# Bucket masks of five groups made in the short convolution, in two-byte form, and their table matmuls in the second convolution layer

## Chip, core and metric

The kernel is one program on one core of a Trainium2 chip. The metric is the device time of one execution in microseconds (us), of which the median of three runs is taken. PE is TensorE, DVE is VectorE, ACT is ScalarE, POOL is GpSimd and SP is SyncE, which issues the loads of weights.

## What is computed

Two networks run one after the other on a sequence of 256 tokens of width 1024: four mixer layers (conformer convolution "a0", forgetting attention "b", short convolution "c", conformer convolution "a1"), then two blocks of token mixer and feed-forward ("m0", "f0", "m1", "f1"). The change touches the first three kinds and one small thing that the token mixers need, the table of position biases. Cut from the reference:

```python
def conformer_conv_mixer(h, w_in, conv_w, conv_b, ln_g, ln_b, w_out):
    val, glu_gate, z = jnp.split(h @ w_in, 3, axis=-1)
    u = causal_depthwise_conv(val * jax.nn.sigmoid(glu_gate), conv_w) + conv_b   # 31 taps
    u = jax.nn.silu(layer_norm(u, ln_g, ln_b))
    return (u * jax.nn.silu(z)) @ w_out

def short_conv_mixer(h, w_in, conv_w, w_out):
    u, b_gate, c_gate, z = jnp.split(h @ w_in, 4, axis=-1)
    y = b_gate * causal_depthwise_conv(c_gate * u, conv_w)                       # 3 taps
    return (y * jax.nn.silu(z)) @ w_out

bias = rel_bias[t5_bucket(q_pos[:, :, None] - k_pos)]      # 32 buckets, 8 heads, in dsa_attention
```

The kernel writes the bias as a sum of steps: for every bucket a mask says whether the distance of a query and a key has reached the bucket's start, and a matmul of the masks with the differences of neighbouring rows of `rel_bias` gives the bias.

## The kernel before

**Pieces.** The weights come as one stream of pieces of 128x1024 (512 KB), loaded by SP into six `raw` buffers in the order of a fixed plan. A "plain" piece is multiplied as it is (fp32, records of `ps<-B,raw`). A "split" piece is first rounded by ACT into one of five `wh` buffers (CAST `wh<-raw`), DVE makes the rest (`wl<-raw,wh`, a TENSOR_TENSOR of 128x1024), and PE multiplies both (`ps<-XS,wh` and `ps<-XS,wl`, 24 matmuls for a piece of an input projection; `ps<-wh,os` and `ps<-wl,os`, 12 for a piece of an output projection). `feed_act` and `feed_dve` call these up to three pieces ahead of the piece that they name. A cast waits for the load and for the matmuls of the split piece that held its `wh` buffer before. Pieces called ada are used by DVE alone (`raw<-raw,cb`), in c and later.

**A conformer layer** (`pe_a`, `act_a`, `dve_a`, `pool_a`) works in eight rounds p = 0 to 7 of 256 channels. In round p PE multiplies the pair g(p) (plain, the gates), the pair v(p) (split from p = 1 on, the values) and, from p = 1, one unit of z (plain up to z3); each round of the plan so has five pieces g, g, v, v, z, and v(p+2).0 takes the `wh` buffer of v(p+1).0. ACT takes the sigmoid (`gate`), DVE multiplies (`val`, `B<-ps,tmp`), and then the round's 31 taps run: ACT scales 12 of them per half (`tmp<-B,C`, in pairs, into three buffers `tmp2` to `tmp4` in turn) and POOL adds them (`B<-B,tmp`, 24 a round), DVE does 17 (`ps<-B,C,ps`, 34 a round) and ends the round with `conv_end` (`B<-ps,B`). ACT and DVE run "items" n = 0 to 29 of a round p, with the work for later pieces put between them by hand: the cast of v(p+1).1 follows item 3, the gate of p+1 item 9, the cast of v(p+2).0 item 13, in even rounds the Silu of z behind it, `stats(p-1)` (a Square, `tmp<-B`) item 17, and the next point used below item 21. ACT has by item 13 scaled five of its twelve taps, by item 21 nine. PE sums the squares in `stats` (`ps<-B,C` and `ps<-tmp,C`, 32x256).

**The table of biases** is made in six groups e = 0 to 5. `masks` on DVE makes four masks y of a group (TENSOR_TENSOR `B<-B`, 128x512), `pe_bias` multiplies them (four matmuls side by side, 32 columns each, `ps<-B,C` 32x512), `act_bias_out` copies the result to `G`, `pe_bias_turn` transposes it (four `ps<-C,G`), and `act_bias` puts it in its place (`B<-ps`, 128x512). Groups 0, 1 and 2 are made in a0 and 3, 4 and 5 in a1: DVE makes four masks ahead of the rounds, and four more in rounds 2 of a0 and 1 and 4 of a1, since all groups use one set of mask buffers and wait for the group before:

```python
            if e:
                dve.wait_ge(*s["table"][e - 1])      # masks: the matmuls of the group before
        if e:
            pe.wait_ge(*s["evac"]["bias", e - 1])    # pe_bias: act_bias of the group before (bank 3)
```

A group's `act_bias` stands one round behind its `pe_bias` in ACT's order, and its turn two rounds behind in PE's.

**The short convolution** c (`pe_c`, `act_c`, `dve_c`) has eight steps i = 0, 2, ... 14 of the pieces c, c, u, u, b, b, o(i-2), z, z, o(i-1), with ada pieces between. DVE multiplies by `ps5` once u is there, runs the taps, multiplies by `ps6` once b is there, and later by the Silu of z; the rests `wl` are fed between these.

## Time and profile before

| | |
|---|---|
| median of three runs (lowest, highest) | 1817.43 us (1815.01, 1819.13) |
| span of the profiled execution | 1817.8 us |
| PE, DVE, ACT, POOL busy | 1747.3, 1446.8, 1075.3, 331.3 us |
| share of the span | 96%, 80%, 59%, 18% |
| mean granted TensorE clock | 0.989 |
| a0, b, c, a1, the rest | from about 0, 245, 521, 756 and 997 us on |

The profiled execution has no time of its own outside the profile; its span lies within the three timed runs. POOL's 18% is an average over a program in which it works in two stretches alone, the rounds of a0 and of a1, so its share there has to be read from windows of these rounds. Busy time of PE counts a matmul from its start to a modelled end, so that 96% says that PE seldom stands still, not that it runs at its peak.

### The profile page before, as it was taken

The numbers are of one execution on the slowest core, as the hardware profiler recorded it, in microseconds if no ns is written. First come the engines' busy times: TensorE is split into PE (matmuls) and PEld (weight loads), VectorE is DVE, ScalarE is ACT, GpSimd is POOL, SyncE is SP. The second block draws the span as 40 slices with busy tenths as digits, with TensorE's granted clock in tenths as the row PEclk, the third lists the DMA queues.
The fourth block names the chain that finished last, engine by engine and source line by source line (L and its number), as shares of the span: only waits on it lengthen the run. The fifth ranks groups of instructions, "written<-read, shape, count | busy, mean of one in ns | idle before, by whom it ended". The sixth has DMA issues, their size and how long they took to land.

```text
span 1817.8 us, 30986 instructions
## 1 busy us (share of the span) xinstructions
PE 1747.3 (96%) x11636; PEld 1580.2 (87%) x11636; DVE 1446.8 (80%) x2710; ACT 1075.3 (59%) x2047; POOL 331.3 (18%) x412
## 2 busy tenths in 40 slices
PE   7998999999999999999989999999999999999997
PEld 6887778888889999988877989989999898989996
DVE  7999777877778878789977688787777778787667
ACT  6888575555454444468975556565555556565554
POOL 2999000000000000079950000020000300030000
PEclk9999999999999999999989999999999999999998
DMA  6444458864558888644335554445764443536552
GB/s 228 150 141 151 140 170 310 275 204 167 197 195 278 301 295 291 208 156 151 132 128 185 169 195 135 166 152 192 242 211 161 154 148 125 176 131 220 190 182 70
DMA packets 92741, 339.62 MB, mean 187 GB/s; under 512 B 10288, under 2 KB 10672, under 8 KB 91952
## 3 DMA queue, kind: packets, MB, share of 16 engines
q1 hardware_dynamic: 92592, 337.64, 55.2%
q8 instruction: 93, 1.52, 0.3%
q14 instruction: 56, 0.46, 0.1%
HBM read 336.55 MB, written 1.05 MB: 186 GB/s over the span
## 4 chain that ended last, share of the span: by engine, by line
PE 62%; DVE 15%; issue 10%; ACT 10%; POOL 2%; DMA 1%; SPq 0%; DVEq 0%; ACTq 0%; POOLq 0%
PE ps L103 60%; DVE wl L119 6%; ACT tmp L109 4%; ACT wh L112 2%; POOL B L119 2%; DVE B L119 2%; PE ps L106 2%; DVE tmp L129 1%; ACT B L109 1%; ACT os L112 1%; DVE raw L129 1%; DVE tmp L119 1%; ACT ps L109 1%; ACT XS L112 1%; DVE os L119 1%
## 5 line engine op out<-in xcount | busy, mean ns | idle before, releaser
L103 PE MATMUL ps<-XS,wh 128*128 128x256 f32 x4464 | 830.2, 288 | 10.6 <-DVE wl L119 9.4
L103 PEld LDWEIGHTS ps<-XS,wh 128*128 128x128 f32 x4464 | 707.4, 194 | 26.5 <-issue 14.3
L119 DVE TENSOR_TENSOR wl<-raw,wh 128x1024 fp32r<-128x1024 f32 x481 | 593.4, 1260 | 111.8 <-ACT wh L112 110.7
L103 PE MATMUL ps<-XS,wl 128*128 128x256 f32 x2232 | 636.1, 285 | 0.0
L112 ACT CAST wh<-raw 128x1024 fp32r<-128x1024 f32 x481 | 486.8, 1045 | 150.2 <-PE ps L103 140.7
L103 PEld LDWEIGHTS ps<-XS,wl 128*128 128x128 f32 x2232 | 432.1, 194 | 0.0
L119 POOL TENSOR_TENSOR B<-B,tmp 128x237 f32<-128x237 f32 (+11 forms) x384 | 287.1, 785 | 644.5 <-ACT tmp L109 644.4
L103 PE MATMUL ps<-wh,os 128*128 128x512 f32 x864 | 284.1, 394 | 12.6 <-DVE os L119 8.4
L129 DVE SCALAR_TENSOR_TENSOR ps<-B,C,ps 128x254 f32<-128x254 f32 (+16 forms) x544 | 211.7, 467 | 6.8 <-ACT ps L109 6.7
L103 PEld LDWEIGHTS ps<-wh,os 128*128 128x128 f32 x864 | 162.4, 188 | 51.9 <-DVE os L119 13.2
L103 PE MATMUL ps<-B,raw 128*128 128x256 f32 x832 | 183.9, 381 | 0.9 <-ACT B L109 0.9
L103 PEld LDWEIGHTS ps<-B,raw 128*128 128x128 f32 x832 | 157.1, 190 | 26.6 <-issue 4.2
L103 PE MATMUL ps<-wh,XS 128*128 128x512 f32 x576 | 179.5, 391 | 0.0
L109 ACT ACTIVATE tmp<-B,C 128x237 f32<-128x237 f32 (+11 forms) x384 | 158.8, 477 | 26.7 <-POOL B L119 26.2
L103 PE MATMUL ps<-wl,os 128*128 128x512 f32 x432 | 168.9, 391 | 0.0
L119 POOL TENSOR_TENSOR X<-X,B 128x512 f32<-128x512 f32 x24 | 44.0, 1848 | 658.0 <-DVE XS L119 657.0
L129 DVE SCALAR_TENSOR_TENSOR tmp<-ps,C,tmp 128x254 f32<-128x254 f32 (+1 forms) x176 | 72.6, 475 | 75.9 <-ACT tmp L109 75.9
L103 PEld LDWEIGHTS ps<-wh,XS 128*128 128x128 f32 x576 | 107.2, 188 | 21.5
L109 ACT ACTIVATE tmp<-ps 128x128 f32<-128x128 f32 (+3 forms) x178 | 73.2, 427 | 77.6 <-PE ps L103 60.8
L129 DVE SCALAR_TENSOR_TENSOR raw<-raw,cb 128x1024 f32<-128x1024 f32 x96 | 116.4, 1218 | 0.0
L109 ACT ACTIVATE tmp<-ps,C 128x256 f32<-128x256 f32 x88 | 44.9, 560 | 117.9 <-PE ps L103 117.9
L103 PE MATMUL ps<-wl,XS 128*128 128x512 f32 x288 | 112.3, 390 | 0.0
(157 smaller groups left out, 1621.6 us busy)
## 6 DMA issues: line engine op xcount, KB each, us to landing
raw<-in_w SPq DMA_DIRECT2D x628, 512.0 KB, 4.4
B<-in_ln SPq DMA_DIRECT2D x4, 1024.0 KB, 6.0
C<-in_cst SPq DMA_DIRECT2D x1, 1103.5 KB, 10.2
X<-in_x SPq DMA_DIRECT2D x2, 512.0 KB, 5.6
out_x<-X SPq DMA_DIRECT2D x4, 256.0 KB, 2.5
cb<-in_cb SPq DMA_DIRECT2D x1, 512.0 KB, 12.8
pos<-in_pos SPq DMA_DIRECT2D x1, 160.0 KB, 2.3
raw<-in_w SPq DMA_DIRECT2D x1, 128.0 KB, 3.0
```

Source lines behind the costliest of these rows:

```text
L103: return NOTHING if self.e is None else self.e.matmul(*a, **k)
L106: return NOTHING if self.e is None else self.e.transpose(*a)
L109: return NOTHING if self.e is None else self.e.activation(*a, **k)
L112: return NOTHING if self.e is None else self.e.copy(*a)
L119: return NOTHING if self.e is None else self.e.tensor_tensor(o, a, b, op)
L129: return self.e.scalar_tensor_tensor(out=o, in0=a, scalar=s, in1=b, op0=op0, op1=op1, **k)
```

## The change

Group 0 stays where it is. The masks of groups 1 to 5 (20 of them) are made in c, one behind each of three places of a step (steps 0 to 12; the last place in steps 0 to 10). All masks are in two-byte form, and every one has a place of its own, so that none waits for a table. The differences of `rel_bias` are split at the start into three two-byte parts, and a group's table is 12 two-byte matmuls in place of 4 in fp32. The tables of groups 1 to 5 are all in a1, group p+1 in round p = 0 to 4: `pe_bias` behind v(p), `act_bias_out` behind item 3 of ACT's round p, the turn behind g(p+1), `act_bias` behind item 21 of the same round p. a0 keeps nothing but group 0.

```diff
@@ -785,31 +785,31 @@
             ins.then_inc(s["sums"].up((A, q)), 1)
 
         def table(p):
-            if p in self.bias_at(j):
-                self.pe_bias_turn(pe, self.bias_at(j)[p], 3)
+            if j and 1 <= p <= 5:
+                self.pe_bias_turn(pe, p, 3)
 
         for p in range(8):
             pair("g", p)
             if j == 0 and p == 0:
                 self.pe_bias_turn(pe, 0, 7)
-            table(p - 2)
+            table(p)
             if p >= 3:
                 stats(p - 3)
             pair("v", p)
-            if p in self.bias_at(j):
-                self.pe_bias(pe, self.bias_at(j)[p], 3)
+            if j and p < 5:
+                self.pe_bias(pe, p + 1, 3)
             if 1 <= p < 7:
                 pair("z", (p - 1) // 2, ((p - 1) % 2,))
         pair("z", 3)
         stats(5)
-        table(6)
         pair("z", 4)
         stats(6)
         pair("z", 5)
         pair("z", 6, (0,))
         stats(7)
         pe.wait_ge(*s["evac"][A, "S"])
-        pe.wait_ge(*s["evac"]["bias", 5 if j else 2])
+        if j:
+            pe.wait_ge(*s["evac"]["bias", 5])
         for b in range(2):
             ins = pe.matmul(self.ps[3][:, b:4:2], self.tmp[4][:, 128 * b:128 * b + 128], self.c("which", 0, 2), start=True,
                             stop=True)
@@ -899,6 +899,8 @@
                 self.feed_act(act, f"{A}.v{p + 1}.1", 0)
             if p == 7:
                 self.feed_act(act, f"{A}.z5.0", 0)
+            if j and p < 5:
+                self.act_bias_out(act, p + 1, 3)
             items(p, 4, 10)
             if p < 7:
                 gate(p + 1)
@@ -910,13 +912,11 @@
             if p in (2, 4, 6):
                 silu_z(p // 2 - 1)
             items(p, 14, 18)
-            if p in self.bias_at(j):
-                self.act_bias_out(act, self.bias_at(j)[p], 3)
             if p:
                 stats(p - 1)
             items(p, 18, 22)
-            if p - 1 in self.bias_at(j):
-                self.act_bias(act, self.bias_at(j)[p - 1], 3)
+            if j and p < 5:
+                self.act_bias(act, p + 1, 3)
             if p >= 6:
                 self.feed_act(act, f"{A}.z{2 * p - 8}.1", 0)
             items(p, 22, 30)
@@ -1004,30 +1004,24 @@
             dve.tt(U[:, a:a + 2, :].rearrange("p a t -> p (a t)"), self.ps[bank["v", p]], self.tmp[p % 2],
                    ALU.mult).then_inc(s["conv"].up((A, "v", p)), 1)
 
-        self.masks(dve, 4)
         self.feed_dve(dve, f"{A}.v1.0", 1)
         val(0)
         for p in range(8):
-            more = 1 if p in ((1, 4) if j else (2,)) else 0
             items(p, 0, 8)
             if p:
                 conv_end(p - 1)
-            self.masks(dve, more)
             if 1 <= p < 7:
                 self.feed_dve(dve, f"{A}.v{p + 1}.1", 0)
             if p == 7:
                 self.feed_dve(dve, f"{A}.z5.0", 0)
             items(p, 8, 14)
-            self.masks(dve, more)
             if p == 7:
                 self.feed_dve(dve, f"{A}.z5.1", 0)
             items(p, 14, 20)
-            self.masks(dve, more)
             if p < 7:
                 val(p + 1)
             self.feed_dve(dve, f"{A}.v{p + 2}.0" if p < 6 else f"{A}.z{2 * p - 8}.0", 0)
             items(p, 20, 28)
-            self.masks(dve, more)
             if p >= 6:
                 self.feed_dve(dve, f"{A}.z{2 * p - 8}.1", 0)
             items(p, 28, 30)
@@ -1150,11 +1144,19 @@
 
     def mask(self, y):
 
-        return self.m["B"][0][:, 2048 + y % 4 * 512:2560 + y % 4 * 512]
-
-    def bias_at(self, j):
-
-        return {0: 3, 3: 4, 6: 5} if j else {1: 1, 4: 2}
+        n = y - 4 if y >= 4 else y
+        if n < 16:
+            place = self.B[1 if y >= 4 and n < 8 else 0][:, 2048 + n % 8 * 256:2304 + n % 8 * 256]
+        elif n < 18:
+            place = self.B[2][:, 3392 + 256 * (n - 16):3648 + 256 * (n - 16)]
+        else:
+            place = self.m["G"][:, 512 + 256 * (n - 18):768 + 256 * (n - 18)]
+        return place.bitcast(BF16)
+
+    def bias_steps(self):
+
+        r = self.m["rep"][3][:].bitcast(BF16)
+        return [r[:, 32 * k:32 * k + 32] for k in range(3)]
 
     def bias_turned(self):
 
@@ -1168,6 +1170,13 @@
         dve.wait_ge(*s["const0"][0])
         dve.tt(self.c("rblk", 0, 32), self.c("rblk", 0, 32), self.c("rblk0", 0, 32), ALU.subtract).then_inc(
             s["bias"].up("steps"), 1)
+        rest = self.c("rblk", 0, 32)
+        for k, o in enumerate(self.bias_steps()):
+            dve.wait_ge(*s["bias"][("rest", k - 1) if k else "steps"])
+            dve.tensor_copy(o, rest).then_inc(s["bias"].up(("part", k)), 1)
+            if k < 2:
+                dve.wait_ge(*s["bias"]["part", k])
+                dve.tt(rest, rest, o, ALU.subtract).then_inc(s["bias"].up(("rest", k)), 1)
         dve.wait_ge(*s["bias"]["pf"])
         dve.ts(pf[:, T:T + 64], pf[:, T:T + 64], self.c("bstart"), None, ALU.add, None).then_inc(s["bias"].up("begin"), 1)
         dve.wait_ge(*s["bias"]["begin"])
@@ -1184,7 +1193,7 @@
             q, g = (0, 16 * e) if e < 2 else (128, 16 * (e - 2))
             g += T + y % 4
             if e:
-                dve.wait_ge(*s["table"][e - 1])
+                dve.wait_ge(*s["table"][0])
             dve.tt(self.mask(y).rearrange("p (c q) -> p c q", c=4),
                    pf[:, q:q + 128].unsqueeze(1).to_broadcast([128, 4, 128]),
                    pf[:, g:g + 13:4].unsqueeze(2).to_broadcast([128, 4, 128]), ALU.is_ge).then_inc(s["mask"].up(y), 1)
@@ -1192,14 +1201,14 @@
     def pe_bias(self, pe, e, bank):
 
         s = self.s
-        pe.wait_ge(*s["bias"]["steps"])
+        pe.wait_ge(*s["bias"]["part", 2])
         for g in range(4):
             pe.wait_ge(*s["mask"][4 * e + g])
         if e:
             pe.wait_ge(*s["evac"]["bias", e - 1])
-        for g in range(4):
-            ins = pe.matmul(self.ps[bank][32 * g:32 * g + 32, :], self.c("rblk", 0, 32), self.mask(4 * e + g), start=True,
-                            stop=True)
+        for k, part in enumerate(self.bias_steps()):
+            for g in range(4):
+                ins = pe.matmul(self.ps[bank][32 * g:32 * g + 32, :], part, self.mask(4 * e + g), start=k == 0, stop=k == 2)
         ins.then_inc(s["table"].up(e), 1)
 
     def act_bias_out(self, act, e, bank):
@@ -1688,6 +1697,7 @@
             dve.wait_ge(*s["gemm"][f"c.u{i}.1"])
             dve.wait_ge(*s["evac"]["c", "c", i])
             dve.tt(cs, self.ps[5], cs, ALU.mult).then_inc(s["evacd"].up(("c", "u", i)), 1)
+            self.masks(dve, 1 if i < 14 else 0)
             for n in range(2):
                 self.feed_dve(dve, f"c.b{i}.{n}")
             dve.wait_ge(*s["evacd"]["c", "u", i])
@@ -1703,6 +1713,7 @@
             dve.wait_ge(*s["gemm"][f"c.b{i}.1"])
             dve.wait_ge(*s["conv"]["c", i + 1, 2])
             dve.tt(ac, self.ps[6], ac, ALU.mult).then_inc(s["evacd"].up(("c", "b", i)), 1)
+            self.masks(dve, 1 if i < 14 else 0)
             if i >= 2:
                 self.feed_dve(dve, f"c.o{i - 2}")
             for n in range(2):
@@ -1714,6 +1725,7 @@
             dve.tt(ac, ac, zs, ALU.mult).then_inc(s["conv"].up(("c", "y", i)), 1)
             for k in range(2):
                 self.dve_low(dve, "c", i + k, ac[:, k * T:k * T + T])
+            self.masks(dve, 1 if i < 12 else 0)
         self.feed_dve(dve, "c.o14")
         self.feed_dve(dve, "c.o15")
 
```

**ACT, round 2 of a1**, from the gate to item 21 (`G<-ps3` is `act_bias_out`, `B2<-ps3` is `act_bias`, `tmp5<-B1` is `stats`; the number behind a name is the buffer's). Before:

```order
L109 ACTIVATE tmp1<-ps4 128x512 [waits s_gemm]
...
L112 CAST wh3<-raw4 128x1024 [waits s_gemm,s_raw4]
L109 ACT_TABLE_LOAD
L109 ACTIVATE B0<-ps7 128x512
...
L109 ACTIVATE tmp5<-B1 128x512 [waits s_sums,s_conv]
...
L109 ACTIVATE tmp4<-B3,C 128x229 [waits s_poolconv]
L109 ACTIVATE tmp4<-B3,C 128x229
L109 ACTIVATE tmp2<-B3,C 128x228 [waits s_poolconv]
```

Now:

```order
L109 ACTIVATE G<-ps3 128x512 [waits s_table]
...
L109 ACTIVATE tmp1<-ps4 128x512 [waits s_gemm]
...
L112 CAST wh3<-raw4 128x1024 [waits s_gemm,s_raw4]
L109 ACT_TABLE_LOAD
L109 ACTIVATE B0<-ps7 128x512
...
L109 ACTIVATE tmp5<-B1 128x512 [waits s_sums,s_conv]
...
L109 ACTIVATE tmp4<-B3,C 128x229 [waits s_poolconv]
L109 ACTIVATE tmp4<-B3,C 128x229
L109 ACTIVATE B2<-ps3 128x8x64 [waits s_turn]
L109 ACTIVATE tmp2<-B3,C 128x228 [waits s_poolconv]
```

Every round from 0 to 4 now has both copies, and `act_bias` stands behind the cast of v(p+2).0 (`wh3`), which waits for the matmuls of v(p+1).0.

**PE, a1, from the end of v(1) to the start of v(2)** (`ps7<-B3,raw3` is the unit of z, `ps5<-B3,raw4` and `raw5` are g(2)). Before:

```order
L103 MATMUL ps4<-XS,wl4 128x256
L103 MATMUL ps7<-B3,raw3 128x256 [waits s_raw3]
L103 MATMUL ps7<-B3,raw3 128x256 x7
L103 MATMUL ps5<-B3,raw4 128x256 [waits s_raw4,s_conv]
L103 MATMUL ps5<-B3,raw4 128x256 x7
L103 MATMUL ps5<-B3,raw5 128x256 [waits s_raw5]
L103 MATMUL ps5<-B3,raw5 128x256 x7
L106 MATMUL ps3<-C,G 128x128 [waits s_evac]
L106 MATMUL ps3<-C,G 128x128 x3
L103 MATMUL ps6<-XS,wh3 128x256 [waits s_low,s_cast]
```

Now:

```order
L103 MATMUL ps4<-XS,wl4 128x256
L103 MATMUL ps3<-B1,rep3 32x512 [waits s_mask,s_evac]
L103 MATMUL ps3<-B1,rep3 32x512 x11
L103 MATMUL ps7<-B3,raw3 128x256 [waits s_raw3]
L103 MATMUL ps7<-B3,raw3 128x256 x7
L103 MATMUL ps5<-B3,raw4 128x256 [waits s_raw4,s_conv]
L103 MATMUL ps5<-B3,raw4 128x256 x7
L103 MATMUL ps5<-B3,raw5 128x256 [waits s_raw5]
L103 MATMUL ps5<-B3,raw5 128x256 x7
L106 MATMUL ps3<-C,G 128x128 [waits s_evac]
L106 MATMUL ps3<-C,G 128x128 x3
L103 MATMUL ps6<-XS,wh3 128x256 [waits s_low,s_cast]
```

The 12 matmuls of a table, of which the first waits for `s_evac` (the `act_bias` of the group before) have come in ahead of z and g; the same rows stand behind v(2), v(3) and v(4), and those behind v(0) without the wait for `s_evac`. Rounds 1 to 5 each have a turn.

**DVE, a step of c**, from the product with `ps5` to the rest of the first z piece, now (before, the same rows without the two `B1<-B2`, which are masks):

```order
L119 TENSOR_TENSOR tmp0<-ps5,tmp0 128x512 [waits s_evac,s_gemm]
L119 TENSOR_TENSOR B1<-B2 128x512
L129 SCALAR_TENSOR_TENSOR raw1,mod<-raw1,cb 128x1024 [waits s_raw1]
L119 TENSOR_TENSOR wl3<-raw2,wh3 128x1024 [waits s_cast]
L129 SCALAR_TENSOR_TENSOR raw3,mod<-raw3,cb 128x1024 [waits s_raw3]
...
L119 TENSOR_TENSOR tmp2<-ps6,tmp2 128x512 [waits s_conv,s_gemm]
L119 TENSOR_TENSOR B1<-B2 128x512
L119 TENSOR_TENSOR wl0<-raw4,wh0 128x1024 [waits s_cast]
```

Both stand ahead of the rest `wl0` of z(i).0, which is the next `wl` that PE needs after the output piece o(i-2). The third mask of a step follows the two `os` of the step's end.

## Rows read from the trace of the kernel before

**Rows 1.** Windows of rounds of a0 and a1: busy us (instructions), clock, DMA.

```profile
69.34:88.74 19.40, 19.22 (x122) 16.34 (x120) 19.40 (x39) 17.11 (x38) 18.72 (x26) 1.00 0.43 143
106.09:127.05 20.96, 20.73 (x122) 18.19 (x121) 18.28 (x43) 16.84 (x38) 17.43 (x26) 1.00 0.45 151
800.78:819.92 19.14, 18.63 (x115) 16.34 (x114) 19.14 (x39) 15.52 (x36) 19.14 (x25) 1.00 0.44 147
819.92:837.28 17.36, 15.09 (x87) 13.17 (x88) 17.36 (x41) 15.57 (x37) 17.36 (x26) 0.90 0.36 122
```

**Rows 2.** Timeline, two POOL additions (a mask, and no mask beside them) and masks on DVE.

```profile
818.83 1.13 POOL L119 TENSOR_TENSOR B<-B,tmp 128x226 f32<-128x226 f32 x1
810.48 0.68 POOL L119 TENSOR_TENSOR B<-B,tmp 128x231 f32<-128x231 f32 x1
...
818.27 1.15 DVE L119 TENSOR_TENSOR B<-B 128x512 f32<-128x512 f32 x1
767.62 2.49 DVE L119 TENSOR_TENSOR B<-B 128x512 f32<-128x512 f32 x4
```

**Rows 3.** Timeline, waits in a0: DVE, PE, ACT, POOL, each [idle <-releaser].

```profile
9.16 0.17 DVE L124 TENSOR_SCALAR sm<-sm 128x2 f32<-128x2 f32 x1 [2.99 <-ACT tmp L109]
93.97 0.36 PE L103 MATMUL ps<-XS,wh 128*128 128x256 f32 x1 [2.09 <-DVE wl L119]
113.85 1.05 ACT L112 CAST wh<-raw 128x1024 fp32r<-128x1024 f32 x1 [2.34 <-PE ps L103]
117.25 34.65 POOL L119 TENSOR_TENSOR B<-B,tmp 128x232 f32<-128x232 f32 x48 [3.53 <-ACT tmp L109]
```

**Rows 4.** Windows behind two waits of PE, and the second wait in the timeline.

```profile
94.00:98.00 4.00, 4.00 (x21) 4.00 (x22) 4.00 (x12) 4.00 (x10) 4.00 (x7) 0.58 0.42 135
882.00:884.00 2.00, 2.00 (x19) 1.97 (x17) 2.00 (x7) 2.00 (x5) 2.00 (x4) 1.00 0.76 254
...
881.06 0.36 PE L103 MATMUL ps<-XS,wh 128*128 128x256 f32 x1 [1.45 <-DVE wl L119]
```

**Rows 5.** Timeline of PE in a1 (z and g, a turn, half of `stats`, a table), and the window of one v pair (v4).

```profile
791.46 10.52 PE L103 MATMUL ps<-B,raw 128*128 128x256 f32 x48
801.82 0.60 PE L106 MATMUL ps<-C,G 128*128 128x128 f32 x4
819.19 0.41 PE L103 MATMUL ps<-B,C 128*32 128x256 f32 x2
829.67 1.06 PE L103 MATMUL ps<-B,C 128*32 128x512 f32 x8
...
841.79:847.81 6.02, 6.02 (x53) 6.02 (x50) 5.32 (x14) 4.10 (x9) 4.37 (x7) 1.00 0.72 264
```

**Rows 6.** Timeline of ACT in rounds 0, 1, 2 and 4 of a1.

```profile
789.47 1.05 ACT L112 CAST wh<-raw 128x1024 fp32r<-128x1024 f32 x1 [2.21 <-DMA raw<-in_w]
808.31 0.61 ACT L109 ACTIVATE tmp<-B 128x512 f32<-128x512 f32 x1
811.33 0.57 ACT L109 ACTIVATE B<-ps 128x512 f32<-128x512 f32 x1
824.81 1.28 ACT L109 ACT_TABLE_LOAD   x1
826.60 1.61 ACT L109 ACTIVATE tmp<-B,C 128x232 f32<-128x232 f32 x4
865.19 1.61 ACT L109 ACTIVATE tmp<-B,C 128x232 f32<-128x232 f32 x4
```

**Rows 7.** Timeline of a step of c, DVE, and the start of z on PE.

```profile
621.19 0.69 DVE L119 TENSOR_TENSOR tmp<-ps,tmp 128x512 f32<-128x512 f32 x1 [1.84 <-PE ps L103]
...
627.20 0.69 DVE L119 TENSOR_TENSOR tmp<-ps,tmp 128x512 f32<-128x512 f32 x1
627.80 3.49 DVE L119 TENSOR_TENSOR wl<-raw,wh 128x1024 fp32r<-128x1024 f32 x3
...
629.50 0.40 PE L103 MATMUL ps<-XS,wh 128*128 128x256 f32 x2
```

## Prediction, made before the changed kernel was run

> **What bounds the kernel now.** I read the stages first (the windows), then who waited for whom in the conformer layers a0 and a1 (waits, timeline), then the chain that ended last, which runs through POOL, ACT and DVE in those two layers and through PE nearly everywhere else.
>
> In the rounds of a0 and a1 POOL is never idle unless it is starved. A round without a mask and without a starving wait takes 17.36 us, and POOL is busy for all of it; a round with four masks takes 19.14, again all busy; two rounds of a0 take 19.40 and 20.96, of which POOL is idle for 0.7 and 3.5 [rows 1]. So POOL's 24 additions a round set the pace, and three things slow them. (1) A mask beside an addition: that addition takes 1.13 us instead of 0.68, and the mask 1.15 instead of its 0.62 (2.49 for four) [rows 2]. (2) DVE, made late by masks, makes `wl` late: PE waits 2.09 us. (3) PE, late, holds back ACT's cast for 2.34 us, and behind the cast stand the taps for which POOL then waits 3.53 us [rows 3]. PE has hardly any slack there: z and g take 10.5 us, a v pair 6.0, `stats` 0.6 (two halves of 0.41 that overlap), so 17.1 of a round's 17.4, and a turn costs 0.5 and a table 1.0 on top (their rows say 0.60 and 1.06, and the next matmul starts within the last part of each) [rows 5]. A wait of PE costs more than itself when it is long: in the 4 us behind the 2.09 us wait the granted clock was 0.58 on average, that is mostly its lower level (1.2 GHz), behind one of 1.45 it stayed 1.00 (2.4 GHz) [rows 4]. 4 us at 0.58 lose 4 x (1 - 0.58) = 1.7; I take 1.5 for such a wait.
>
> In c PE has no idle time, and DVE's chain is short of slack at one place of each step (below).
>
> **Start.** Five small operations on the 32 columns of `rblk` come ahead of the first masks, and the first table becomes two-byte. The small operation of this stage on DVE takes 0.17 us, so five that wait for each other take about 1.0 by my estimate, and DVE then stands idle for 2.99 before ACT's squares are there [rows 3]: hidden, 0. It would take five operations of 0.6 to get past that.
>
> **a0: 8 masks, 2 tables, 2 turns, 4 copies go.** The four masks ahead of the rounds stand where DVE waits for PE or ACT anyway: 0. The four in round 2 cost POOL 4 x 0.45 = 1.8 us, and the idle 0.7 goes too: the round falls from 19.40 to 17.36. Round 4's 3.53 us wait came from PE being 2.34 late. PE gets earlier by the 2.09 wait, the slow stretch of 1.5, two tables of 1.0 and a turn of 0.5, 6.1 in all; ACT asks 2.0 earlier; 6.1 - 2.0 exceeds 2.34, so the wait goes and the round falls from 20.96 to 17.36. Sum -2.0 - 3.6 = **-5.6 us**. What follows the rounds waits for them and moves as a whole. Bounds: -2.0 if another wait takes the place of the second, -5.8 if the last idle 0.15 goes too.
> The Trainium skill (SBUF — State Buffer, "Who interferes with whom") says that a DVE operation with two SBUF inputs and a GpSimd operation that reads SBUF share a port, and that the loser is blocked until the other is done; the trace agrees in kind, 1.13 against 0.68. By that rule a mask could cost POOL its full 0.62 and not 0.45, and a0 would win 0.7 us more. I keep the row.
>
> **c: 20 masks of 0.62 us come.** POOL is idle here, so nobody shares. DVE's step has idle time (1.84 us before the product with `ps5`), but between 621.8 and the end of the first `wl` of three at about 629.0 there is next to none: the rows follow each other, and PE starts on that `wl` at 629.50 [rows 7]. Two masks stand in this stretch, 1.25 us against a slack of 0.5. PE is late by about 0.65 (0.55 to 0.75, slack of other steps being up to 0.2 more), and since DVE's next product waits for PE again, every step pays anew. Step 0 has no output piece and is looser; steps 2 to 12 pay: 6 x 0.65 = **+4 us**. Bounds: 0 if the slack is larger than the rows show, +7.5 if nothing hides. The third mask falls into a wait for a cast (under 0.1).
>
> **a1: 12 masks go, 3 tables become 5, 3 turns 5, 6 copies 10.** Without anything new this would gain: four masks fewer in round 1 and in round 4 (19.14 to 17.36). But `act_bias` of group p+1 now stands in ACT's round p behind the cast of v(p+2).0, and PE's table of group p+2, right behind v(p+1), waits for it. The cast itself waits for v(p+1).0 on PE. So there is a closed chain: table, z and g, turn, `stats`, v(p+1).0, cast, taps six to nine with the Square among them, `act_bias`, next table. I take 0.7 for a two-byte table. No row shows one; the four 32-column groups of an fp32 table plainly run side by side (1.0 us for four matmuls of 512 columns), so three parts should stand between a part's 0.25 x 3 and the fp32 price. Bounds: 0.65 (a little under the row's 1.0), and 12 x 0.25 = 3.0 if the twelve run one after another.
>
> ACT, from the start of the cast at time c: 0.95 to the next instruction, four pairs of taps at 0.77 (1.61 for four taps, two pairs), the Square 0.5, `act_bias` 0.5 = 5.0; in even rounds the table load and Silu of z add 1.8 (824.81 to 826.60) [rows 6]. PE, from table to the end of v(p+1).0: 0.7 + 10.5 + 0.5 + 0.6 + 3.0 = 15.3. One turn of the chain so takes 20.3 us in an odd round and 22.1 in an even one, against 17.4 now.
> - Round 0: the cast starts at 789.2 (789.47 now [rows 6]; g(1), whose end releases its load, ends 0.3 earlier with the cheaper table). Round 0 has no Square, so `act_bias(1)` ends at 789.2 + 0.95 + 3.1 + 0.5 = 793.7. PE ends v(1) at 791.8 (z now starts at 791.46 [rows 5], less 0.3 and with a turn of 0.5 ahead), and waits 1.9 us.
> - The cast of round 1 starts at 793.7 + 0.7 + 10.5 + 0.5 + 3.0 = 808.4, that of round 2 at 808.4 + 20.3 = 828.7, of round 3 at 828.7 + 22.1 = 850.8, of round 4 at 850.8 + 20.3 = 871.1.
> - In each PE, which ends v(p+1) 3.0 us behind c, waits for `act_bias`: 2.0, 3.8 and 2.0 us.
> - Round 4's taps go on at 871.1 + 0.95 + 1.8 = 873.9, now 865.19 [rows 6]: 8.7 late. The rest of the round no longer holds three masks, 3 x 0.45 = 1.35. **+7.4 us**.
> - The clock: the wait of 3.8 us surely lets it fall, +1.5. The three of 1.9 to 2.0 lie between 1.45 (no fall) and 2.09 (fall); I count one, +1.5. Together **+3 us** (1.5 to 6).
> After group 5 nothing waits like this, and rounds 5 to 7 are as before. So a1 loses 10.4 us. Serial tables would add 4 x 2.3 = 9.
>
> **Sum**: 1817.8 - 5.6 + 4 + 10.4 = 1826.6, made against the profiled span of 1817.8, which is 0.4 above the median: I predict **1826.5**.
>
> **Rivals.**
> 1. *The chain in a1 doesn't close*, because PE is later at v(p+1), or ACT earlier at item 21, than I have it. It decides at the wait of PE's table: if that is under some 0.5 us. For it: today the copy at `act_bias`'s place in round 1 ends at 811.9 [rows 6] and PE's v(2) at 808.7 (819.19 - 10.5 [rows 5]), so the closeness rests on a few us, and the chain has a dozen links. Against it: all links are in the order of both engines, and PE would have to lose over 2 us elsewhere. a1 would then gain at best 1.8 + 2.8 for rounds 1 and 4, less what two more turns and five tables take of PE's time, say 4: 1817.8 - 5.6 + 4 - 4 = 1812. This is the one on the other side.
> 2. *c hides its masks.* For it: DVE is idle for a fifth of c. Against: that time lies elsewhere in the step. 1826.6 - 4 = 1822.5.
> 3. *The two-byte tables run one after another*: 1835.
> 4. *Half a chain*: PE waits in one or two rounds only, as the even rounds' Silu is the only long link; a1 +2, in all 1818, no change.
>
> **How the numbers follow.** Forecast as summed, 0.55; c hides, 0.18; serial tables, 0.05; half a chain, 0.08; chain open, 0.14. Likeliest case's own range is 1822 to 1832 (a1's clock term and c's bounds). The range for all leaves out the open chain and the upper half of the serial case: **1816 to 1833**. A measurement of this kernel can tell about 0.2% from no change, 3.6 us: faster means below 1813.8, slower above 1821.1. Faster 0.13, same 0.10, slower 0.77.
>
> **What would show it.** Right: POOL's rounds of a0 all near 17.4 but the first and the last two; in a1 PE waits before `ps<-B,rep` (the new table) in rounds 1 to 4 for `B<-ps` on ACT, 1.9, 2.0, 3.8 and 2.0 us; ACT's casts there wait for PE, rounds 1 to 4 take 19 to 24 us and show clocks under 1.00; in c PE waits about 0.65 us for `wl` at the start of z in six steps; the table takes 0.7. Wrong: no wait before the tables (the a1 term changes its sign), no waits of PE in c (4 us less), or rounds of a0 that still show a starved POOL.

## The result, and the profile after

| | before | after |
|---|---|---|
| median (lowest, highest) | 1817.76 us (1815.01, 1819.13), 4 runs | 1832.66 us (1830.57, 1833.71), 4 runs |
| ratio | | 1.0083, 95% interval 1.0068 to 1.0097 |
| profiled span | 1817.8 us | 1831.3 us |

The change makes the kernel slower by 0.83%, 14.9 us; 1826.5 were predicted, 9 us slower, with 1816 to 1833 as the range. The result lies 0.3 us inside the end of that range, and 0.7 us above the likeliest case's own range of 1822 to 1832.

To see where the time went, the span is cut at VectorE's first addition of each layer's result to `X` (`X<-X,ps` in the timeline). Each number below is the distance between two such starts in one profiled execution, in us; the first begins at 0 and the last ends with the span. The kernels with a number are the experiments further down.

| kernel | a0 | b | c | a1 | rest |
|---|---|---|---|---|---|
| before | 244.34 | 275.89 | 235.45 | 239.28 | 822.88 |
| after | 238.73 | 275.92 | 240.17 | 253.97 | 822.54 |
| e1, copy at the gate | 240.97 | 275.90 | 240.17 | 236.02 | 821.31 |
| e2, copy behind the cast | 239.47 | 275.83 | 240.16 | 237.15 | 822.47 |
| e3, masks in DVE's waits | 239.11 | 275.84 | 235.43 | 253.71 | 821.28 |
| e4, both moves | 237.70 | 275.86 | 235.45 | 235.94 | 821.21 |
| e5, form alone | 243.36 | 275.86 | 235.44 | 235.34 | 821.26 |
| e6, masks back in a0 | 241.33 | 275.90 | 240.18 | 254.74 | 821.27 |
| e7, copy two taps earlier | 238.09 | 275.86 | 240.18 | 242.74 | 822.42 |
| e8, both and a later cast | 244.07 | 275.90 | 235.44 | 237.71 | 821.25 |
| e9, one mask ahead of z | 238.51 | 275.96 | 237.16 | 253.02 | 822.47 |
| e10, three masks ahead of z | 238.14 | 275.89 | 243.12 | 253.77 | 822.56 |
| e11, both, one part | 240.03 | 275.87 | 235.44 | 235.55 | 822.45 |

So a0 gave back 5.6 us, c took 4.7 more and a1 14.7 more. c repeats to 0.02 us between kernels that have the same c. a0 does not: between after, e1 and e2, which are the same program there, it differs by 2.2. A difference of one or two us in a0 or a1 is therefore not read as an effect unless the rounds show it.

Most of that scatter lies behind the rounds (and up to 1.6 us of it ahead of those of a0). From the end of POOL's last addition to the first addition to `X`, a layer of this kind takes 60.7, 61.7 or 63.1 us, in whatever kernel, and the granted clock of that stretch is 1.00, 0.97 or 0.95. It falls to 0.50 for some us shortly behind the rounds. Whether it does goes with how long PE waits for ACT 1.6 us behind POOL's last addition, and that differs between executions: after waits 0.39 us there in a0 and keeps its clock, e1, the same program up to there, waits 1.51 us and shows the longest stretch. The stretch behind the rounds of a0 and of a1, in before, in after and (a0 alone) in e1, with its length, the busy time of each engine and its number of instructions, the granted clock and the DMA:

```profile
core 0: us, PE busy (x) PEld busy (x) DVE busy (x) ACT busy (x) POOL busy (x), PEclk, DMA share, GB/s
182.66:244.34 61.68, 56.47 (x284) 46.54 (x283) 46.83 (x71) 38.76 (x61) 0.01 (x1) 0.97 0.45 146
932.00:994.97 62.97, 57.05 (x276) 47.28 (x277) 46.60 (x70) 38.12 (x60) 0.00 (x0) 0.95 0.46 149
178.03:238.73 60.70, 55.52 (x287) 45.48 (x286) 46.74 (x70) 38.66 (x61) 0.00 (x1) 1.00 0.47 147
947.15:1008.79 61.64, 56.45 (x283) 46.49 (x282) 46.59 (x69) 38.13 (x60) 0.00 (x0) 0.97 0.49 151
177.82:240.97 63.15, 57.39 (x279) 47.45 (x278) 46.82 (x70) 38.78 (x61) 0.00 (x0) 0.95 0.45 142
```

POOL's stretch, from its first addition in a layer to its last, leaves this out. In a0 it went from 149.24 to 144.67 us, 4.6 less (the other 1.0 of the 5.6 is the clock behind the rounds); in a1 it went from 150.93 to 166.95, 16.0 more (the clock behind the rounds hides 1.3 of that). Kernels with the same a0 agree in it to 0.8 us.

The rounds come first, as in [rows 1]: two of a0 (2 and 4), then rounds 0 to 4 of a1.

```profile
69.49:87.49 18.00, 16.98 (x104) 15.01 (x104) 17.33 (x40) 16.27 (x37) 17.33 (x25) 1.00 0.47 147
104.82:122.42 17.60, 17.12 (x105) 15.05 (x104) 16.93 (x40) 16.15 (x37) 17.44 (x25) 1.00 0.49 150
780.20:800.64 20.44, 17.34 (x105) 14.81 (x104) 15.72 (x39) 14.37 (x36) 16.31 (x24) 0.92 0.33 104
800.64:822.14 21.50, 18.70 (x119) 16.57 (x118) 17.10 (x40) 15.44 (x37) 17.35 (x26) 1.00 0.40 126
822.14:844.79 22.65, 18.21 (x114) 15.10 (x113) 17.38 (x40) 17.35 (x39) 17.33 (x26) 0.92 0.33 114
844.79:867.26 22.47, 20.02 (x122) 16.95 (x121) 16.85 (x40) 16.74 (x38) 17.43 (x25) 0.92 0.36 118
867.26:891.53 24.27, 24.05 (x139) 21.20 (x139) 17.38 (x40) 17.37 (x39) 17.36 (x25) 1.00 0.49 152
```

In a0 the round of 19.40 us is now 18.00 and that of 20.96 is 17.60. In a1 POOL is busy for 17.4 us of a round as before, but rounds 1 to 4 last 21.5 to 24.3: it is starved for four to seven us in each. The granted clock is 0.92 in three of them. What PE waits for there, from its timeline of 790 to 843 us:

```profile
794.05 1.37 PE L103 MATMUL ps<-B,rep 128*32 128x512 bf16 x12 [3.10 <-ACT B L109]
816.06 0.83 PE L103 MATMUL ps<-B,rep 128*32 128x512 bf16 x12 [2.80 <-ACT B L109]
838.83 1.47 PE L103 MATMUL ps<-B,rep 128*32 128x512 bf16 x12 [4.44 <-ACT B L109]
```

And the waits by line (total, times, longest) of 780 to 930 us:

```profile
PE ps L103 <- ACT B L109: 13.3, 6, 4.4
```

`ps<-B,rep` is the two-byte table, and the wait ahead of it is for ACT's copy of the table before. Three of the four are here; the fourth, at 861.09, is 2.45. A table takes 0.83 us, and 1.37 or 1.47 when the clock falls with it. ACT's side, round 1, to be held against [rows 6]:

```profile
807.11 0.60 ACT L109 ACTIVATE tmp<-ps 128x512 f32<-128x512 f32 x1 [2.84 <-PE ps L103]
807.61 0.86 ACT L109 ACTIVATE tmp<-B,C 128x233 f32<-128x233 f32 x2
810.83 1.05 ACT L112 CAST wh<-raw 128x1024 fp32r<-128x1024 f32 x1 [2.37 <-DMA raw<-in_w]
811.78 1.62 ACT L109 ACTIVATE tmp<-B,C 128x232 f32<-128x232 f32 x4
813.31 0.61 ACT L109 ACTIVATE tmp<-B 128x512 f32<-128x512 f32 x1
813.83 1.60 ACT L109 ACTIVATE tmp<-B,C 128x230 f32<-128x230 f32 x4
815.34 0.57 ACT L109 ACTIVATE B<-ps 128x512 f32<-128x512 f32 x1
```

Read it as a loop. The table of 794.05 delays PE's g, whose end lets both the sigmoid (807.11) and a load go; the cast waits for that load until 810.83; behind it stand four tap pairs and the Square; the copy ends at 815.9, and the table of 816.06 starts at once. In rounds 2 to 4 the same cast waits for `ps` on PE (831.61, 855.86, 878.33, each 2.77 us), not for the load.

In c, PE now waits for `wl` in six steps, as the waits of 535 to 750 us say:

```profile
PE ps L103 <- DVE wl L119: 3.2, 6, 0.7
```

A wait of PE and a step of DVE, from the timeline, for [rows 7]:

```profile
567.62 0.48 PE L103 MATMUL ps<-XS,wh 128*128 128x256 f32 x2 [0.51 <-DVE wl L119]
...
623.78 0.69 DVE L119 TENSOR_TENSOR tmp<-ps,tmp 128x512 f32<-128x512 f32 x1
624.39 0.68 DVE L119 TENSOR_TENSOR B<-B 128x512 bf16<-128x512 f32 x1
624.99 3.49 DVE L119 TENSOR_TENSOR wl<-raw,wh 128x1024 fp32r<-128x1024 f32 x3
```

The mask (`B<-B`, bf16) stands straight ahead of the three residues for which PE waits.

### The profile page after: what moved, and what is told of

It is laid out like the page before. It is cut to its first block, busy times and chain, and to the rows that moved or that the text cites. A ratio compares the mean times of both kernels' runs of the same rounds, so it can differ in the third digit from the quotient of the medians.

```text
span 1831.3 us, 31038 instructions
## 1 busy us (share of the span) xinstructions
PE 1747.8 (95%) x11660; PEld 1577.9 (86%) x11660; DVE 1443.4 (79%) x2715; ACT 1076.0 (59%) x2047; POOL 326.6 (18%) x412
## 4 chain that ended last, share of the span: by engine, by line
PE 58%; DVE 17%; issue 12%; ACT 9%; POOL 3%; DMA 1%; SPq 0%; DVEq 0%; ACTq 0%; POOLq 0%
PE ps L103 56%; DVE wl L119 7%; POOL B L119 3%; ACT tmp L109 3%; ACT wh L112 2%; DVE B L119 2%; DVE tmp L129 2%; PE ps L106 2%; DVE raw L129 1%; DVE tmp L119 1%; ACT os L112 1%; ACT B L109 1%; ACT XS L112 1%; ACT ps L109 1%; DVE os L119 1%
## 5 line engine op out<-in xcount | busy, mean ns | idle before, releaser
L119 POOL TENSOR_TENSOR B<-B,tmp 128x237 f32<-128x237 f32 (+11 forms) x384 | 282.4, 776 | 664.3 <-ACT tmp L109 664.1
L129 DVE SCALAR_TENSOR_TENSOR ps<-B,C,ps 128x254 f32<-128x254 f32 (+16 forms) x544 | 211.7, 467 | 12.1 <-ACT ps L109 11.9
## 6 DMA issues: line engine op xcount, KB each, us to landing
C<-in_cst SPq DMA_DIRECT2D x1, 1103.5 KB, 10.2
```

The lines of the kernel that those rows point to most:

```text
L119: return NOTHING if self.e is None else self.e.tensor_tensor(o, a, b, op)
L129: return self.e.scalar_tensor_tensor(out=o, in0=a, scalar=s, in1=b, op0=op0, op1=op1, **k)
```

## Experiments

Theory: each term has its own place. In a1 a closed chain, table, g, cast, copy, next table, paces the rounds; in c two masks ahead of the residues of z are late; in a0 the masks and tables that left are the gain. Rival: the added work itself (12 products, a turn and two copies a round; 20 masks) or the two-byte form costs the time wherever it stands.

**e1, the copy at the gate.**

```diff
                 gate(p + 1)
+                if j and p < 5:
+                    self.act_bias(act, p + 1, 3)
...
             items(p, 18, 22)
-            if j and p < 5:
-                self.act_bias(act, p + 1, 3)
```

> The changed kernel with one call moved: the copy of each turned table out of the bank (act_bias) stands right behind the sigmoid of the next gate, some 4 to 9 us earlier in each round of a1, so that it no longer depends on the cast of the value weights. Theory of the closed chain (table p+2 waits for that copy, the copy for the cast, the cast for the transfer, the transfer for the products that the last table delayed): PE's waits before the tables vanish, POOL's span in a1 falls from 167.0 us back to about 151 to 153, the rest stays (a0 5.6 us shorter than before, c 4.7 longer), and the time is 1817 to 1820 us. Rival, load: twelve products, four turns, and two ScalarE copies more in each of rounds 0 to 4 cost the time themselves; then a1 stays above 160 us and the time above 1827.

Measured 1815.5 us (12 runs), 0.9993 of before (0.9979 to 1.0006), somewhat below the 1817 to 1820 expected. a1 fell from 253.97 to 236.02, POOL's part of it from 167.0 to 150.0. The waits of PE in 780 to 930 us:

```profile
PE ps L103 <- ACT B L109: 0.5, 2, 0.3
```

Neither of the two stands before a table. All products, turns and copies are still there, so the load is refuted as the cause and the chain is shown: one call, moved up by twelve items, took back 17 us of the rounds of a1 and 17 of the time. c kept its 240.17.

**e2, the copy behind the cast.** The same call directly behind the cast of v(p+2).0.

> The changed kernel with the same call moved half as far: right behind the cast of the next pair's value weights, ahead of four tap pairs and the Square. It stays behind the cast and its wait for the transfer, and loses some 3 to 4 us of ScalarE work behind it. Theory of the closed chain: the waits before the tables were 2.5 to 4.4 us, so most of them vanish or fall below 1 us, and the loop still exists but closes with little or nothing over: a1 gives back 10 to 15 of its 14.7 us, time 1818 to 1823. If it is the cast's wait for the transfer and not the sum along the chain that holds the table, the waits stay at 1.5 us or more and the time stays above 1826. Rival, load: no change, 1832.

Measured 1816.66 us (12 runs), 0.9994 (0.9981 to 1.0008), where 1818 to 1823 were expected; a1 took 237.15, 16.8 less than after, where 10 to 15 less were expected.

```profile
PE ps L103 <- ACT B L109: 1.0, 2, 0.7
```

Neither of these two waits stands before a table either. The cast with its own wait is still in the loop, and the loop no longer closes. What made it bind was the 3.6 us of taps and Square (811.78 to 815.34 above) between cast and copy.

**e7, two tap pairs only.** The dose between: the copy ahead of items 18 to 21.

```diff
-            items(p, 18, 22)
             if j and p < 5:
                 self.act_bias(act, p + 1, 3)
+            items(p, 18, 22)
```

> The changed kernel with the copy of the turned table ahead of the two last tap pairs that stood before it (four activations, 1.60 us), still behind the cast and the Square. A dose for the closed chain: each of its four turns is 1.6 us shorter, so PE's waits of 3.1, 2.8, 4.4 and 2.5 us fall to some 1.5, 1.2, 2.8 and 0.9, half of their sum, and a1 gives back 6 to 10 of its 14.7 us; time 1823 to 1827. If the time is that of the copy behind the cast (about 1816.7), the loop closes by less than 1.6 us a turn. Rival, load: 1832.

Measured 1823.83 us (10 runs), 1.0026 (1.0007 to 1.0046). a1 took 242.74, 11.2 less than after.

```profile
PE ps L103 <- ACT B L109: 6.2, 6, 2.8
```

Four of these stand before tables (0.80, 1.15, 2.82 and 0.94), 5.7 us in place of 12.8, where 6.4 were expected: 6.4 us less in the loop (4 x 1.60) took away 7.1 us of waiting. So the loop answers to its length, about one to one. The clock fell behind one of the four waits, not behind three, which is worth another 3.2 us; together that is the 10.2 us by which POOL's stretch in a1 got shorter (156.71 for 166.95). The profiled execution is the fastest of the ten; by the medians the kernel gave back 8.8 us, within the 6 to 10 expected.

**e3, the masks of c in DVE's waits.**

```diff
                 self.feed_dve(dve, f"c.c{i}.{n}")
+            self.masks(dve, 1 if i < 14 else 0)
             for n in range(2):
                 self.feed_dve(dve, f"c.u{i}.{n}")
+            self.masks(dve, 1 if i < 14 else 0)
             dve.wait_ge(*s["gemm"][f"c.u{i}.1"])
...
+            self.masks(dve, 1 if i < 12 else 0)
             dve.wait_ge(*s["evac"]["c", "z", i])
```

The three calls at the old places are taken out.

> The changed kernel with the three masks of a step of c put where VectorE waits in the kernel before: one ahead of the residue of u's weights, one ahead of the wait for u's product, one ahead of the wait for the silu of z. Theory: the 4.7 us that c grew come from two masks that stood ahead of the residues of z's weights, so PE's waits of 0.5 us at z vanish and c comes back by 3.5 to 4.7 us; a1 stays; time 1828 to 1829. Rival, amount or contention (20 masks of 1.15 us slow VectorE or the memory wherever they stand): less than 1.5 us come back, time above 1831.

Measured 1827.18 us (7 runs), 1.0052 (1.0034 to 1.0070); 1828 to 1829 were expected. c took 235.43, before 235.45: the same 20 masks cost nothing there. PE's six waits for `wl` at z are gone.

**e9 and e10, the dose in c.** Of the two masks ahead of z's residues one is moved to the end of the step (e9), or the third is put beside them (e10).

> The changed kernel with one of the two masks that stood ahead of the residues of z's weights in c (the one behind the product with ps6) put at the end of the step; a1 untouched. The dose of the c term downward: one mask of 0.62 us against a slack of some 0.5 to 0.7. Theory: PE's wait at z is 0.1 us or less and c, from its first addition to X to that of a1, takes 235.4 to 236 us instead of 240.2 (235.45 before). Rival, every mask in c costs its share: 238 to 239.

> The changed kernel with the third mask of a step put ahead of the residues of z's weights too, so that three stand there; a1 untouched. The dose upward: PE's wait at z grows from 0.5 by the mask's 0.62 to 1.1 us in six steps, and c takes 240.2 + 6 x 0.62 = 243.9 us at least, up to 245 if a step loses again more than the wait shows. Rival: 240.2, since the count of masks is the same.

One run each, 1828.90 and 1835.29 us. c took 237.16 (e9), 240.17 (after, two masks) and 243.12 (e10), against 235.45. Waits of PE in 535 to 750 us in e9:

```profile
PE ps L103 <- DVE wl L119: 0.5, 1, 0.5
```

and in e10:

```profile
PE ps L103 <- DVE wl L119: 6.3, 6, 1.3
```

Both missed their numbers. e10 has the third mask there in five of the six paying steps only, as the last mask runs out: 5 x 0.61 = 3.05, and 2.95 were measured; the expectation counted six. e9 was to be free and cost 1.7. Set against before, step for step, its products with `ps5` lose 0.68 us in the first step (the wait of 0.5), 0.35 in one and 0.13 to 0.14 in each of the five others, in which the profile shows no wait of PE (last section). The 0.68 are not of z: the two masks that now stand at the end of the first step are ahead of the next residue there, and PE waits for that one at 553.03:

```profile
549.32 1.29 DVE L119 TENSOR_TENSOR B<-B 128x512 bf16<-128x512 f32 x2
```

So with one, two and three masks ahead of z's residues, c loses 1.0, 4.7 and 7.7 us there, at an unchanged count of masks: the further the residues are pushed, the more c takes.

**e4, both moves.** e1 and e3 in one kernel.

> Both moves in one kernel. If the two costs are separate and the 5.6 us that a0 gained stand by themselves, the time is that of before less 5.6 and up to 1 us of what is left in c and a1: 1811 to 1815 us, faster than before by 0.2 to 0.35%. If the load is the cause in either place, it stays above 1822.

Measured 1813.09 us (12 runs), **0.9964 of before (0.9950 to 0.9978)**, the fastest of the kernels that compute the whole table. Its profiled execution, 1807.96 us, is one of its fastest, so its parts in the table above sum to less than its median. Rounds 0 to 4 of its a1:

```profile
774.40:793.85 19.45, 19.45 (x123) 17.26 (x122) 15.36 (x39) 14.38 (x36) 16.32 (x24) 1.00 0.43 136
793.85:811.62 17.77, 17.77 (x115) 15.79 (x114) 17.11 (x40) 15.34 (x37) 17.30 (x26) 1.00 0.48 151
811.62:831.45 19.83, 19.83 (x129) 17.09 (x129) 16.85 (x40) 17.33 (x39) 17.46 (x25) 1.00 0.48 156
831.45:849.50 18.05, 17.45 (x117) 14.74 (x116) 16.74 (x40) 16.62 (x38) 17.42 (x25) 1.00 0.40 125
849.50:868.69 19.19, 18.96 (x116) 16.73 (x115) 17.25 (x40) 17.33 (x39) 17.37 (x26) 1.00 0.47 161
```

PE is busy for 93.5 of 94.3 us, at the full clock: with the loop open PE itself, not POOL, looks like the bound.

**e11, one part of three.** To test that, each table is made from the first part alone (4 products for 12), so its values lack their lower digits.

> Both moves, and each table from the first of the three parts of the steps alone: four products instead of twelve, so the table lacks its lower digits. In the kernel with both moves TensorE has 0.8 us of idle time in the 91 us from the first table of a1 to the fifth, so I take it for the bound there. Theory: a table falls from 0.83 us to about 0.39, the next product starts 0.42 to 0.45 earlier, and the POOL rounds 0 to 4 of a1 shrink by 4 to 5 such pieces, 1.7 to 2.2 us, from 94.3 us. Rival: ScalarE's taps and GpSimd bound those rounds, and they stay at 94 us.

One run, 1811.15 us. A table took 0.40 us, and rounds 0 to 4 together 92.93 us: 1.4 less, where 1.7 to 2.2 were expected and the products freed 5 x 0.43 = 2.2. Rounds 1 and 3 did not move (17.81 and 18.06), and a wait of PE for ACT's copy to `G` grew from 0.60 to 0.94. How rounds 0 and 2 share the rest can't be read: e1, which has the same a1 as e4, took 20.30 and 18.99 us for them where e4 took 19.45 and 19.83, with the same sum of all five (94.3). So PE is the bound in part only; in the odd rounds something else is, which no run here names. The time of one run says nothing beside e4's (1807.48 to 1814.37).

**e5, the form alone**, on the kernel before: masks in two bytes, three parts, 12 products, all at the old places.

> The kernel before with the two-byte form alone: masks written in two bytes, the steps of the table split in three parts, twelve products for four; masks and tables stay where they were. Theory (places decide, not the form): a mask away from GpSimd takes 0.69 us in four bytes and 0.68 in two, a table 1.06 and some 0.8 to 1.4, so the time stays within 0.2% of before. If the four-byte writes are what slowed GpSimd beside a mask, rounds 2 of a0 and 1 and 4 of a1 fall by 0.5 to 1.4 us each and the time by 2 to 3 us. Rival, form costs: the tables take longer and the chain that ends a0 and a1 grows, time over 1821.

Measured 1816.32 us (12 runs), 0.9985 (0.9967 to 1.0003): no difference that can be told. Round 2 of a0 and rounds 1 and 4 of a1, the ones with masks:

```profile
69.86:88.99 19.13, 19.06 (x120) 16.11 (x119) 19.13 (x39) 17.07 (x38) 18.70 (x25) 1.00 0.46 144
799.67:818.80 19.13, 18.48 (x114) 16.19 (x114) 19.13 (x39) 15.51 (x36) 19.13 (x26) 1.00 0.47 147
853.54:873.63 20.09, 19.86 (x125) 16.91 (x123) 20.09 (x43) 17.08 (x38) 19.41 (x26) 1.00 0.45 153
```

Round 4 of a1 in before, for the last of them:

```profile
856.35:876.45 20.10, 19.88 (x125) 16.93 (x123) 20.10 (x41) 17.07 (x38) 18.68 (x25) 1.00 0.45 151
```

In a1 19.13 and 20.09 us, where before had 19.14 and 20.10; in a0 19.13 for 19.40, but e6 below takes the same 19.13 there with four-byte masks. So a mask beside POOL's additions costs the same in two bytes as in four. The form is neither the cost nor the gain.

**e6, the masks back in a0.** Eight four-byte masks, read by nobody, at the places that before had, on the changed kernel.

```diff
+        if j == 0:
+            self.copies(dve, range(4))        # ahead of the rounds
...
+            if more:                          # round 2 of a0, at the four old places
+                self.copies(dve, (n,))
```

> The changed kernel with eight four-byte masks made again in a0 where the kernel before made them (four ahead of the rounds, four in round 2), without tables behind them, and read by nobody. It splits the 5.6 us that a0 gained. Theory: round 2 goes from 18.0 us back to 19.4 and the rest of the gain (round 4, where a table stood behind the copy of the last one) stays, so GpSimd's end in a0 lies 1.3 to 2 us later than in the changed kernel, 3 us ahead of before. Rival: the masks are all of it, and the end of a0 is back by 4.6 us or more. The time is near 1834.

Measured 1836.41 us (6 runs), 1.0094 (1.0066 to 1.0121). Rounds 2 and 4 of a0:

```profile
68.75:87.88 19.13, 17.85 (x114) 15.31 (x114) 19.13 (x39) 16.73 (x37) 19.13 (x26) 1.00 0.44 138
105.19:125.00 19.81, 19.58 (x117) 17.16 (x116) 17.87 (x43) 16.34 (x37) 17.40 (x26) 1.00 0.49 160
```

Round 2 came back as expected, round 4 did not stay at 17.6: without any table it takes 19.81 again, since its cast waits for its load:

```profile
111.80 1.05 ACT L112 CAST wh<-raw 128x1024 fp32r<-128x1024 f32 x1 [2.22 <-DMA raw<-in_w]
```

PE was late there because the masks had made VectorE late. Its waits in 70 to 115 us of e6 (0.4 us in after):

```profile
PE ps L103 <- DVE wl L119: 3.5, 2, 2.3
```

POOL's stretch in a0 is 149.24 us before, 147.82 here and 144.67 after. Of the 4.6 us the masks are 3.2 and the tables with their turns and copies 1.4, from one execution each, with 0.8 us of scatter between kernels of the same a0: expectation (1.3 to 2) and rival (4.6) both fell, and the truth lies between them.

**e8, a later cast**, an attempt at more: e4 with the cast of v(p+2).0 behind item 17 in place of 13.

> Both moves, and the cast of the next pair's value weights two tap pairs later in each round of a0 and a1: in rounds 2 and 4 of a1 that cast still held ScalarE for 1.2 us until a unit of TensorE freed its buffer, and GpSimd, which lives on ScalarE's taps, waited 1.9 us behind it. If taps go ahead of the wait, GpSimd's idle time in those rounds falls by 1 to 2 us each, 1809 to 1812 us. Rival: the value weights come later, TensorE waits for their residue, and the time is that of both moves (1813) or above.

Measured 1814.71 us (12 runs), 0.9978 (0.9958 to 0.9997): not the 1809 to 1812 expected, and by the time not to be told from e4, as the intervals overlap. The rounds say that nothing was gained: POOL's stretch took 147.48 us in a0 for e4's 144.29, and 150.64 in a1 for 149.92. POOL's first rounds got shorter (16.27 for 18.61 us in round 0 of a0), but then its rounds 4 and 5 of a0 took 20.7 and 20.4: PE had to wait for the residue that the later cast delays, and in the four us behind the wait its granted clock was 0.50. The row of PE's waits in 60 to 185 us:

```profile
PE ps L103 <- DVE wl L119: 4.3, 1, 4.3
```

## Why the prediction held, and where it was off

The sum came out 6.2 us low, and that the time still lies in the range, by 0.3 us, is in part luck. Between the two profiled executions the change costs 13.5 us, 4.7 more than the 8.8 summed: 4.3 in a1 and 0.7 in c, in the sizes and not in the mechanism. The other 1.4 are the base. In every run that lists both, a time is 1.7 to 1.9 us longer than its span, so the 1817.8 of before are a time of about 1819.6, which is 1.8 above the median and not 0.4, where after's execution is 0.5 above its own.

**Start, 0.** The five small operations on `rblk` took 0.18 to 0.19 us each, the masks start 1.1 us later, DVE still stands idle for 1.89 us behind them (2.99 before), and POOL starts its first round at 33.36 us (33.42 before).

**a0, -5.6.** Measured -5.60 to the addition to `X`, -4.6 to the end of POOL's rounds; the other 1.0 is a clock behind the rounds that was fuller than in before's execution, so the match to the last digit is luck. Round 2 fell to 18.00 and not to 17.36, since POOL kept an idle time of 0.67; what a mask costs POOL held (19.13 us busy with four masks in e6, 17.33 without, so 0.45 each). The step that failed is the split: "PE gets earlier by the 2.09 wait, the slow stretch of 1.5, two tables of 1.0 and a turn of 0.5" made the tables part of why round 4 recovers. e6 shows that the masks alone bring round 4 back to 19.8; only about 1.1 us of it belonged to what PE and ACT no longer do.

**c, +4.** Measured 4.72. "PE is late by about 0.65, 6 x 0.65" was right in place and in the count of steps; five steps cost 0.73 and one 0.96, and the first 0.08. The prediction's own 1.25 - 0.5 = 0.75 was nearer than the 0.65 that it took. e3 shows the cause: the same masks elsewhere cost nothing.

**a1, +10.4.** Measured 14.7, and 16.0 in the rounds, the largest error. The mechanism held, and e1, e2 and e7 show it. The sizes: the waits before tables 2 to 5 were 3.1, 2.8, 4.4 and 2.5 us where 1.9, 2.0, 3.8 and 2.0 were predicted, 3.1 more. Set against the prediction's own links, the 5.6 us that the rounds took beyond their forecast are these:

- The clock, 1.8. I counted two falls (+3); it fell behind three of the four waits and lengthened z and g by 3.6 us together (11.7, 10.6, 11.5 and 12.3 us, each from the first to the last of its products, for 10.6 at full clock) and two tables by 1.2, in all 4.8.
- PE's part of the loop, from a table's start to the next cast's, 1.2. It took 15.1, 15.6, 15.5 and 15.6 us without the clock's share, where 14.7 and three times 15.3 were summed. In round 1 "The cast itself waits for v(p+1).0 on PE" was the shorter arm: the cast waited for its load, which the end of g releases. A table takes 0.76 us to the start of z, where I had 0.7; three quarters of a us was already the lower end of the prediction's own reasoning (0.25 x 3).
- ACT's part, from the cast's start to the next table's, 0.9: 5.2, 7.2 and 5.2 us for 5.0, 6.8 and 5.0.
- The first wait, 1.2. The first table that waits starts 13.85 us behind POOL's first addition of a1, where 12.6 were predicted; the cast of round 0 had waited 3.19 us for its load, 2.21 in before. Why that load landed later stays open.
- The rest, 0.5, lies behind the last cast.

The links without the clock were each short by 0.2 to 0.4 us only; the closed loop adds them up.

**The gain under the chain.** I took it that with an open chain a1 would gain 4 us, 1812 in all, with c's cost still there. e1 is that kernel: 1815.5 us, and POOL's stretch in a1 is 149.96 for 150.93 in before, 1.0 less. But e5, with the masks still in a1, took 149.26. The difference to before lies in round 3 (17.39 us for 19.07), behind a round 2 that before's execution ran at a granted clock of 0.90. So no run shows that the masks' leaving gains anything in a1. The 3.3 us by which the table above has e4's a1 below before are 1.0 in the rounds and 2.3 behind them, where the clock was 0.95 in before and 1.00 in e4.

The Trainium skill (SBUF — State Buffer, "Who interferes with whom") was cited for the port that DVE and GpSimd share: e5's masks away from POOL took 0.69 us and beside it up to 1.16, so the trace agrees in kind, and it does so for two-byte output too.

## What to carry to other kernels

When work is packed closer in a loop that two engines run by hand, write down the one operation that hands a buffer back (here the copy out of the bank) and count what stands ahead of it in its engine's order from the last thing that it depends on through the other engine: if that sum with the other engine's part exceeds a round, the loop sets the pace, and moving one cheap instruction frees it. Extra work on an engine with idle time is not free everywhere: 20 masks cost 4.7 us where two of a step stood ahead of residues that another engine needs at once, and nothing where there was slack behind them. Here that was in front of the waits. A cost per turn of a loop has to be summed with care, since an error in it comes back with every turn; and two executions are compared by the stretch that the change touches, since the clock of an untouched stretch can differ by more than the effect.

## What the runs showed that was not expected

**A wait costs more than its idle time, even at the full clock.** In c six waits of 0.5 to 0.7 us sum to 3.2, but c took 4.7 more, and the granted clock stayed at 1.00. Start to start, the products of PE follow at 0.23 us (512 columns) while each record lasts 0.39, so idle time counted from the end of a record leaves out 0.16 us of overlap that is lost too, and the first product behind a gap is followed after 0.19 us, where it is 0.11 in before and 0.12 between the others. 0.16 + 0.07 + 0.50 = 0.73, the step's loss (to a hundredth). The rows behind the wait of 0.72:

```profile
625.25 0.39 PE L103 MATMUL ps<-wh,os 128*128 128x512 f32 x1
626.36 0.47 PE L103 MATMUL ps<-XS,wh 128*128 128x256 f32 x2 [0.72 <-DVE wl L119]
626.66 0.28 PE L103 MATMUL ps<-XS,wl 128*128 128x256 f32 x1
```

From 625.25 to 626.36 are 1.11 us, where before has 0.23: 0.88 lost, and 0.72 shown. The steps of e9 that lost 0.14 us show no wait at all, and their loss is in the starts:

```profile
595.79 0.39 PE L103 MATMUL ps<-wh,os 128*128 128x512 f32 x1
596.09 0.47 PE L103 MATMUL ps<-XS,wh 128*128 128x256 f32 x2
```

The two starts are 0.29 us apart (596.09 and 595.79 are rounded) for 0.23, and the next product follows after 0.19 for 0.11: 0.06 + 0.08 = 0.14.

**The clock's answer to a wait is not fixed by its length.** In after the granted clock was 0.57 in the four us from 794 on, behind a wait of 3.10, and 0.60 from 838.8 on, behind 4.44; from 816 on, behind one of 2.80, it was 1.00:

```profile
838.80:842.80 4.00, 3.97 (x20) 2.54 (x21) 2.48 (x7) 3.19 (x10) 4.00 (x7) 0.60 0.00 0
816.00:820.00 4.00, 3.94 (x27) 3.09 (x28) 3.90 (x11) 3.19 (x10) 4.00 (x7) 1.00 0.00 0
794.00:798.00 4.00, 3.95 (x19) 2.54 (x20) 3.77 (x11) 2.75 (x8) 4.00 (x7) 0.57 0.00 0
```

In e7 a wait of 2.82 us was followed by z and g of 12.1 us for 10.6, and one of 2.45 in after by 12.3. So among waits of 2.4 to 3 us both outcomes occur, and a forecast can only give them a share. Behind the rounds shorter waits went with a fall: none did where PE waited up to 0.72 us there, it came behind 0.85 us in before's a0 (61.7 us) and behind 2.33 us in its a1 (63.0), but not behind 1.11 us in e5's a0 (60.7). PE stands still there a second time, for 0.49 us, in every kernel.

**Twelve two-byte products of 32 columns on four column groups took 0.83 us**, against 1.06 for four in fp32 [rows 5]: three times the products in less time. To the start of the next product it is 0.76 us against 1.00.
